# Third expert stage: gate and up in four column tiles at once, both halves of down at once, and units one after another

## The reference

```python
h = jax.nn.silu(xs @ w_gate) * (xs @ w_up)      # 1024 -> 512, twice
y = (h * combine_weight) @ w_down               # 512 -> 1024
```

## Time and profile before

| | |
|---|---|
| median of 3 runs | 1347.6 us (1338.69 to 1348.74) |
| profiled execution | 1346.59 us, of it 1344.7 us span |
| third expert stage in the trace | from about 860 us (gather of group 0) to 1332 us |
| TensorE busy, share of the span | 91% |
| DMA traffic in the third stage | 427 to 430 GB/s |
| mean granted TensorE clock | 0.940 of full speed |

### The profile page before, as it was taken

The page is one execution under the profiler, slowest core; times in us unless marked ns, Lnnn a source line. Parts: engine busy times, 40 slices in busy tenths (PEclk is TensorE's granted clock), DMA queues, the critical chain, the costliest instruction groups (busy, mean ns, idle before and its releaser), DMA issues.

```text
span 1344.7 us, 14544 instructions
## 1 busy us (share of the span) xinstructions
PE 1228.6 (91%) x5866; PEld 616.3 (46%) x5866; DVE 319.7 (24%) x891; ACT 204.9 (15%) x468; POOL 1.0 (0%) x6
## 2 busy tenths in 40 slices
PE   6999998999999998999899999898898898899885
PEld 3547545555358765655346554522332242232221
DVE  1325425111300254311232274410010001000002
ACT  2013422101100351110113131100000000000000
POOL 0000000000000000000000000000000000000000
PEclk8997588999999798999989999899999999999998
DMA  9783003699954203499935331199999999999993
GB/s 350 144 296 122 1 3 124 265 416 418 383 205 143 108 1 125 185 407 414 382 119 192 126 118 63 63 385 427 428 427 429 429 428 429 428 428 426 428 428 144
DMA packets 76872, 364.38 MB, mean 271 GB/s; under 512 B 21234, under 2 KB 26644, under 8 KB 52116
## 3 DMA queue, kind: packets, MB, share of 16 engines
q1 hardware_dynamic: 75876, 361.93, 67.6%
q10 hardware_dynamic: 944, 1.73, 0.3%
HBM read 362.60 MB, written 1.05 MB: 270 GB/s over the span
## 4 chain that ended last, share of the span: by engine, by line
PE 74%; DMA 18%; DVE 4%; issue 2%; ACT 1%; SPq 0%; DVEq 0%; ACTq 0%
DMA weights<-in_expert_w_down_dram 17%; PE bank L953 13%; PE bank L993 9%; PE bank L659 9%; PE bank L696 6%; PE bank L674 5%; PE bank L986 4%; PE bank L687 4%; PE bank L1017 3%; PE bank L925 2%; PE bank L928 2%; PE bank L759 1%; PE bank L733 1%; PE bank L893 1%; DMA weights<-in_ab_w_in_dram 1%
## 5 line engine op out<-in xcount | busy, mean ns | idle before, releaser
L953 PE MATMUL bank<-weights,projected 128*64 128x256 f32 (+1 forms) x2048 | 342.6, 491 | 22.0 <-DMA weights<-in_expert_w_gate_dram 10.6
L953 PEld LDWEIGHTS bank<-weights,projected 128*64 128x64 f32 (+1 forms) x2048 | 134.8, 124 | 215.3 <-issue 170.5
L993 PE MATMUL bank<-weights,work 128*32 128x512 f32 x512 | 121.3, 629 | 29.5 <-DMA weights<-in_expert_w_down_dram 28.9
L659 PE MATMUL bank<-weights,x_transposed 128*128 128x512 f32 (+1 forms) x288 | 121.4, 579 | 10.0 <-DMA weights<-in_ab_w_in_dram 6.8
L659 PEld LDWEIGHTS bank<-weights,x_transposed 128*128 128x128 f32 x288 | 54.6, 193 | 70.5 <-issue 65.2
L993 PEld LDWEIGHTS bank<-weights,work 128*32 128x32 f32 x512 | 34.7, 115 | 113.6 <-issue 112.9
L696 PE MATMUL bank<-weights,mixed 128*128 128x512 f32 x192 | 84.3, 596 | 1.6 <-DVE mixed L1768 1.1
L674 PE MATMUL bank<-x_transposed,weights 128*128 128x256 f32 (+1 forms) x336 | 73.3, 380 | 0.0
L1954 DVE COPY work<-bank 128x512 f32<-128x512 f32 (+1 forms) x32 | 22.1, 690 | 207.2 <-PE bank L993 139.5
L674 PEld LDWEIGHTS bank<-x_transposed,weights 128*128 128x128 f32 (+1 forms) x336 | 62.3, 186 | 11.6 <-issue 2.0
L1017 PE MATMUL bank<-work,heads_transposed 128*128 128x512 f32 x128 | 63.7, 620 | 0.0
(11 more groups left out here) (287 smaller groups left out, 1044.4 us busy)
## 6 DMA issues: line engine op xcount, KB each, us to landing
weights<-in_expert_w_gate_dram SPq DMA_DIRECT2D x32, 2048.0 KB, 16.2
weights<-in_expert_w_up_dram SPq DMA_DIRECT2D x32, 2048.0 KB, 17.3
weights<-in_expert_w_down_dram SPq DMA_DIRECT2D x32, 2048.0 KB, 17.2
weights<-in_moe_w_gate_dram SPq DMA_DIRECT2D x16, 2048.0 KB, 10.4
weights<-in_moe_w_up_dram SPq DMA_DIRECT2D x16, 2048.0 KB, 12.3
weights<-in_moe_w_down_dram SPq DMA_DIRECT2D x16, 2048.0 KB, 8.8
weights<-in_sb_w_in_dram SPq DMA_DIRECT2D x6, 2048.0 KB, 17.8
weights<-in_w_in_dram SPq DMA_DIRECT2D x6, 2048.0 KB, 14.7
```

Of the source, the lines that this page charges most:

```text
L659: i = mm(BANK[4 + 2 * (seq % 2) + t][:, 0:ncols], XT[:, kt, t * P:(t + 1) * P], w[:, kt, :], start=kt == 0, stop=kt == KT - 1)
L953: i = mm(b[n_slots * c:n_slots * (c + 1), e * F:(e + 1) * F], x[:, kt, q * n_slots:(q + 1) * n_slots], w[c][:, col:col + F], start=kt == 0 ...
L993: i = mm(BANK[2 + half][r0 + n_slots * c:r0 + n_slots * (c + 1), :], hT[:, a * step + f, n_slots * c:n_slots * (c + 1)], slot(n + c)[:, co ...
```

## The change

The chunks of a unit now follow each other without overlap of units: gate, up, down of unit 0, then of unit 1, and so on. A new function `hidden_both` waits for the four chunks of gate and up and computes both in one series: per block of 128 rows, gate of the two experts in column tiles 0 and 1 (bank 0, partitions 0 to 63) and up in tiles 2 and 3 (bank 1, partitions 64 to 127). Gate and up give their four slots back at the end of the series. `down` works through both halves in one series, one in each pair of tiles, with the same two banks. The copies out of PSUM read and write other partitions, to fit. The number of MATMULs is the same. The two other expert stages keep their order and work. The core of the diff:

```diff
 def expert_order(units):
 
+    if units > 1:
+        return [(kind, u) for u in range(units) for kind in ("gate", "up", "down")]
     order = []
...
+                    def hidden_both(u):
+
+                        w = [load(kind, u) for kind in ("gate", "up")]
+                        for kt in range(KT):
+                            for k in range(2):
+                                for c in range(2):
+                                    q = 2 * u + c
+                                    r0 = rows * k + n_slots * c
+                                    i = mm(BANK[k][r0:r0 + n_slots, :], x[:, kt, q * n_slots:(q + 1) * n_slots],
+                                           w[k][c][:, kt * F:(kt + 1) * F], start=kt == 0, stop=kt == KT - 1)
+                                    if kt == KT - 1:
+                                        i.then_inc(chunk_done, 1)
+
...
                         else:
-                            r0 = rows * (u % 2) if quads else 0
                             for f in range(step):
-                                for c in range(2):
-                                    col = (a * step + f) * D + half * CH
-                                    i = mm(BANK[2 + half][r0 + n_slots * c:r0 + n_slots * (c + 1), :],
-                                           hT[:, a * step + f, n_slots * c:n_slots * (c + 1)],
-                                           slot(n + c)[:, col:col + CH], start=f == 0, stop=f == step - 1)
+                                for hh in range(2):
+                                    for c in range(2):
+                                        r0 = rows * ((u + hh) % 2) + n_slots * c
+                                        col = f * D + hh * CH
+                                        i = mm(BANK[2 + hh][r0:r0 + n_slots, :], hT[:, f, n_slots * c:n_slots * (c + 1)],
+                                               slot(n + c)[:, col:col + CH], start=f == 0, stop=f == step - 1)
+                                    if f == step - 1 and hh == 0:
+                                        i.then_inc(y_psum, 1)
+                            i.then_inc(chunk_done, 2)
+                            return
...
+                    for s_ in (xc_act, xc_dve):
+                        pe.wait_ge(s_, g * (gathers // 2) + (gather0 // 2 + gathers // 2))
+                    if units > 1:
+                        for u in range(units):
+                            if u:
+                                pe.wait_ge(h_ready, g * units + (unit0 + u))
+                            hidden_both(u)
+                            if u == 0:
+                                transposed_weights()
+                                pe.wait_ge(pwT_act, g + (G * L + 1))
+                            if u == units - 1 and not last:
+                                gather(g + 1, lambda: hidden_T(u))
+                            else:
+                                hidden_T(u)
+                            down(u, 0, 0)
+                            scatter(u, 0, 0)
+                            scatter(u, 0, 1)
+                        return
...
-                        if u:
-                            outputs(g, u - 1)
+                        r0 = rows if units > 1 else 0
+                        ac(SG[r0:r0 + rows, :], BANK[0][0:rows, :], ACT.Silu).then_inc(silu_done, 1)
+                        if units > 1 and u < units - 1:
+                            outputs(g, u)
```

More of the change, by code:

```diff
@@ L973, in down @@
                         if a == 0 and u == units - 1 and not last:
-                            pe.wait_ge((xc_act, xc_dve)[half], g * (gathers // 2) + (gather0 // 2 + gathers))
+                            for s_ in (xc_act, xc_dve) if quads else ((xc_act, xc_dve)[half],):
+                                pe.wait_ge(s_, g * (gathers // 2) + (gather0 // 2 + gathers))
                         n = n0 + first_chunk(units, "down", u)
@@ new lines, in transposed_weights @@
+                    def transposed_weights():
+                        pe.wait_ge(p_ready, g * 2 + (2 * G * L + 2))
+                        blocks = WP // P
+                        for block in range(blocks):
+                            for t in range(T):
+                                i = nc.tensor.transpose(BANK[2 + block // 2][:, (block % 2) * S + t * P:(block % 2) * S + (t + 1) * P],
+                                                        PW[:, t * WP + block * P:t * WP + (block + 1) * P], ident)
+                            if block % 2 or block == blocks - 1:
+                                i.then_inc(pwT_psum, 1)
@@ L1050, in group @@
+                    hidden("gate", 0)
+                    transposed_weights()
+                    hidden("up", 0)
                     u = units - 1
@@ L1446, in group @@
                             act.wait_ge(h_ready, g * units + (unit0 + u))
-                        ac(SG[0:rows, :], BANK[0][0:rows, :], ACT.Silu).then_inc(silu_done, 1)
-                        if u:
-                            outputs(g, u - 1)
+                        r0 = rows if units > 1 else 0
+                        ac(SG[r0:r0 + rows, :], BANK[0][0:rows, :], ACT.Silu).then_inc(silu_done, 1)
+                        if units > 1 and u < units - 1:
+                            outputs(g, u)
                     if not last:
@@ L1953, in outputs @@
                     r0 = rows * (pair % 2) if rows < P else 0
-                    cp(YS[r0:r0 + rows, (pair // 2 if rows < P else pair) % 2, 1, :], BANK[3][r0:r0 + rows, :]).then_inc(y_dve, 1)
+                    from0 = rows - r0 if rows < P else 0
+                    cp(YS[r0:r0 + rows, (pair // 2 if rows < P else pair) % 2, 1, :], BANK[3][from0:from0 + rows, :]).then_inc(y_dve, 1)
                 def transposed(g, u):
@@ L1958, in transposed @@
                     by_f = lambda w: w.rearrange("p (f s) -> p f s", f=4)
-                    cp(by_f(HT[:, 0:4 * rows]), by_f(BANK[0 if u == units - 1 else 2][:, :])[:, :, 0:rows]).then_inc(hT_ready, 1)
+                    r0 = rows if units > 1 else 0
+                    cp(by_f(HT[:, 0:4 * rows]), by_f(BANK[0 if u == units - 1 else 2][:, :])[:, :, r0:r0 + rows]).then_inc(hT_ready, 1)
                 def group(g, last):
@@ L1968, in group @@
                     for u in range(units):
-                        if u:
-                            transposed(g, u - 1)
                         dve.wait_ge(silu_done, g * units + (unit0 + u + 1))
                         dve.wait_ge(chunk_done, g * per_group + (n0 + first_chunk(units, "up", u) + 2))
-                        tt(HB[0:rows, :], SG[0:rows, :], BANK[1][0:rows, :], ALU.mult).then_inc(h_ready, 1)
-                        if u:
-                            outputs(g, u - 1)
+                        r0 = rows if units > 1 else 0
+                        tt(HB[r0:r0 + rows, :], SG[r0:r0 + rows, :], BANK[1][r0:r0 + rows, :], ALU.mult).then_inc(h_ready, 1)
+                        if u < units - 1:
+                            transposed(g, u)
+                            outputs(g, u)
                     if last:
```

## The result

| | before | after |
|---|---|---|
| median of 4 runs each, same chip | 1348.2 us (1338.7 to 1359.4) | 1381.9 us (1373.0 to 1395.2) |
| ratio, 95% interval | | 1.025 [1.014, 1.037] |
| profiled execution, its span | 1346.6, 1344.7 us | 1376.1, 1374.3 us |
| mean granted TensorE clock | 0.940 | 0.885 |
| TensorE busy, share of the span | 91% | 79% |

What follows compares the result with a forecast made beforehand. Weight transfers were taken to bound the third expert stage. The profiled 1346.6 us, plus 0 for the start and 28.0 for the handovers, less 1.3 for the tail, gave 1373.3 us, range 1344 to 1390.

Steps and rivals of the forecast that it cites:

- What bounds the kernel: Third expert stage: weight transfers at 427 to 429 GB/s bound it, so TensorE time saved inside is worth nothing by itself.
- The work on TensorE: Third expert stage: joint series 7.06 us instead of 14.1, down 3.6 instead of 7.06, 169 us off TensorE.
- (a): Start of the third stage's weight stream: first series ends at the same time as before, so 0 us.
- (b): Weight stream: the queue runs dry at 14 handovers between units, 2.0 us each, +28.0 us.
- E: Time from the last up chunk's landing to the joint series' end: 9.2 us, of which 2.0 from the low clock.
- The lower bound of 0.8 us: Least loss per handover between units, with the series ending 8.8 us after up's landing and half the queue's start hidden.
- (c): Work behind the last weight chunk: shorter down and copies at the same time, -1.3 us.
- Rival 1: Third stage: the stream never stops if the series ends under about 8.2 us after up's landing; 1345.3 us, chance 0.13.
- rival 2: Joint series run at 1.2 GHz from end to end, 14.1 us each, 7.0 us a handover; 1443 us, chance 0.05.
- rival 3: Joint series: the four tiles don't run at once, 9.0 us a handover; 1473 us, chance 0.04.
- rival 4: Third stage: TensorE's 47.6 us of weight waits were on the path, so faster, down to 1299 us; chance 0.03.
- The signs named: Profile after, third stage: about 400 GB/s, units of 31.4 us, series of 8.5 to 10, up waits of some 10.

Runs made afterwards that it cites:

- e1: Changed kernel with unread matmuls (11, 9, 12 and 4 calls) filling TensorE's wait between the series; 1381.7 us, 1.026 times before.
- e7: Changed kernel with more unread matmuls (12, 10, 15 and 5 calls) filling TensorE's wait between the series; 1369.0 us, 1.015 times before.
- e2: Changed kernel with gate and up apart again, each behind its own two chunks, units still not overlapping; 1346.2 us, 0.9995 times before.
- e3: Kernel before with only down in four column tiles, both halves at once; 1346.7 us, 1.000 times before.

## Why the prediction was right, step by step

**What bounds the kernel: right.** TensorE's busy time fell by 128 us in the stream's stretches and nothing came of it.

**The work on TensorE: right.** The joint series takes 7.08 us at full clock (e1 and e7, rows above), 7.06 forecast; down takes 3.64, 3.6 forecast. Over the stage they averaged 9.03 and 68.0 / 16 = 4.25 us because of the low clock.

**(a) Start, 0: right for the change.** The first joint series took as long as the gate series before, and the issue came right behind it:

```profile
859.40 7.07 PE L968 MATMUL bank<-weights,projected 128*32 128x512 f32 x64 [1.18 <-DVE projected L1970]
866.61 0.92 SPq L535 DMA_DIRECT2D weights<-in_expert_w_gate_dram  x2
```

The -9.0 us of the profiled pair is scatter of the early stages. It hides part of the loss: stream and tail together cost 41.7 - 3.1 = 38.6 us, where the forecast had 28.0 - 1.3 = 26.7. So the nearness of 1373 to the pair's 1376.1 is partly luck. The ratio of the runs, 1.4 to 3.7% or 19 to 49 us, takes in both.

**(b) The stream: the mechanism was right, its size too small.** Forecast 28.0; the 14 handovers cost 36.5, or 2.61 each instead of 2.0. The 0.6 is made up of three differences:

- E was 9.35 on average, against 9.2, which adds 0.15: the low clock lasted 2.7 to 6.0 us into a series, around the 4.1 assumed.
- From the end of the series to the landing of the next gate took 7.8 to 8.2 us at 13 handovers and 9.6 at one, 8.1 on average, against the 7.5 of the earlier trace rows, which adds 0.6. Of that, 0.16 is between the end and the issue (899.88 to 900.04), and the rest a restart of 7.7 to 8.0.
- The last down chunk landed 9.95 us after up on average, not 9.8, which takes 0.15 off again.

Two remarks beside the sum were wrong:

- That nothing is lost below E = 8.2 us, with 1.5 us of backlog, and the step "9.2 is near 9.8" that follows from it. At full clock 0.6 us was lost with 2.6 us of backlog. By the line through the rows the loss begins at E = 6.6, which leaves 9.8 - 6.6 = 3.2 us.
- The lower bound of 0.8 us was named as "half of the start hidden", but 8.8 + 7.5 - 14.7 less half of 2.6 is 0.3. The losses after the change were 1.6 to 3.5 us, so the upper bound of 3.0 was the one that was too tight for single handovers.

The estimate by the Trainium skill ("DMA: Bandwidth & Descriptors", section "Anatomy of one DMA — SWDGE (gpsimd) path"), a fixed cost of about 2.0 us given for the GpSimd path, would have given 1.4 us a handover; on SyncE's queue the trace shows 7.9 - 4.9 = 3.0 us for a restart, and the measurement decides.

A further 5.2 us was nowhere in the sum: six single chunks inside a unit landed 0.6 to 1.4 us late. At each such place a 16 KB fetch of instructions had run 2 to 6 us before (at 921.7, for one, with the late landing at 923.8). In the kernel before, the five later fetches of 16 KB ran beside the unbroken stream and left no mark on its landings; one at 883.6, when the stream had just started, was followed by a chunk that landed 1.5 us late, as the one at 874.6 was after the change. So it was in e2 and e3, whose streams are unbroken too. A fetch seems to cost time where the queue has just been empty. This is argued from the times alone and wasn't tried.

**(c) The tail, -1.3: right in sign, -3.1 measured.** The end of the kernel after:

```profile
1342.62 8.50 PE L968 MATMUL bank<-weights,projected 128*32 128x512 f32 x64 [16.36 <-DMA weights<-in_expert_w_up_dram]
...
1352.54 0.75 PE L980 MATMUL bank<-consts,work 128*128 128x128 f32 x4 [1.42 <-DVE work L2001]
1353.80 3.64 PE L1010 MATMUL bank<-weights,work 128*32 128x512 f32 x32 [0.52 <-DVE work L1987]
1358.12 3.70 PE L1037 MATMUL bank<-work,heads_transposed 128*128 128x512 f32 x8 [0.68 <-ACT work L1462]
```

The last down chunk landed at 1353.2, 10.7 us after up instead of 9.8, and the last series needed only E = 8.6. So down began 0.6 us behind the landing, where 2.3 had been forecast.

**The rivals.** Rival 1, a stream that never stops, didn't happen: its bound of E, 8.2 us, was too generous, and E came out above it at 8.5 or more. The series were never wholly at 1.2 GHz (rival 2: 9.03 us on average, not 14.1), the four tiles did run at once (rival 3), and the waits of TensorE were not on the path (rival 4). On rival 2 the Trainium skill ("TensorE: Matmul & The Clock Gate", section "HAM oscillation — how this bites in real kernels") says that each burst between waits for DMA starts throttled and that the cost is paid once a burst. The trace of the kernel after agrees: the 14 series ahead of a handover began at 0.50, and each was back at full clock before its end.

**The signs named.** GB/s was 390 (about 400 named); a unit with its handover took 29.4 + 2.6 = 32.0 us (31.4 named); the series 8.4 to 10.0 us (8.5 to 10); SyncE waited for line 968, as said; TensorE's waits for up were 185.8 / 15 = 12.4 us each (some 10 named).

## What to carry to other kernels

Where transfers bound a stage, price a merged step by when it gives its buffers back, not by the engine time it saves: here 128 us less of TensorE bought nothing, and four slots held by one step cost 36.5 us of stream. Compare the time from the last landing to the release with the transfers still under way, less some 3 us (here 3.2) for the end and the restart of the queue. Count the idle time that the faster step makes as well: it lowered the clock of the very series on which the next issue waited.

## What was not expected of the hardware

- **A queue needs its next issue well before it is empty.** Down's last chunk was marked as landed at 900.4, but the 16 DMA engines didn't run out together. Two us before the landing most of them had nothing left:

```profile
898.00:899.00 1.00, 1.00 (x16) 0.39 (x12) 0.00 (x0) 0.00 (x0) 0.00 (x0) 1.00 0.08 33
899.00:900.00 1.00, 0.89 (x12) 0.00 (x0) 0.00 (x0) 0.00 (x0) 0.00 (x0) 1.00 0.04 16
```

  And the issue at 900.04 moved nothing before 901. So the bytes all but end some 2 us before the landing is signalled and begin 1 us after the issue, about the 3.2 us of backlog that the table of losses asks for.
- **Short idle times brought the low clock.** After 3.37 us of idling a series of e1 took 8.77 us; after 2.15 and 2.26 us such a series took 7.08. In the kernel before, a wait of 2.73 us had done it. The length alone doesn't decide: in e1 a series after 2.34 us took 8.59, and one after 2.89 us took 7.07.
- **Four column tiles run at full rate for long.** 64 matmul records in 7.08 us are 16 rounds of four at about 0.43 us, the rate of two tiles, with streams from four slots at once.
